# Pooling and convolution-norm stores moved to ScalarE, margin-only zeroing, and the first projection's first tile formed inside its norm

## The reference: what is computed

```python
# first block, per layer
h = layer_norm(x) * (1 + scale) + shift          # scale, shift: rows of a modulation  silu(c) @ mod_w + mod_b
u = h @ w_in                                     # 33 tiles of 128 columns: pooling, rwkv, hgrn, gate
y_pool = pooled average minus u, times pool_w, pool_scale
# second block, first layer
h = rms_norm(x) * (1 + scale) + shift ;  u = h @ w_in
y_a = silu(layer_norm(dwconv(a_val * sigmoid(a_gate))))      # "conformer" part, 512 channels
q, k = axial_rope(rms_norm(q)), axial_rope(rms_norm(k))      # 5 tiles of 128 rows, latent and context
# later modulations: silu(c_2) @ w_ada + b_ada  (3072 columns for each of two layers)
```

## Time and profile before

| | us |
|---|---|
| median of 3 runs | 5943.3 |
| the profiled execution, its own time | 5948.01 |
| span of the profile | 5946.2 |
| TensorE busy | 5146.7 (87%) |
| VectorE busy | 3381.0 (57%) |
| ScalarE busy | 1907.4 (32%) |
| GpSimd busy | 1754.7 (30%) |

### The profile page before, as it was taken

How to read it: one execution, slowest core, us unless ns; L and a number is a source line. 1 busy time by engine, 2 the same in 40 slices (tenths; PEclk the granted TensorE clock), 3 DMA queues, 4 the chain that set the end, 5 groups by cost and what they waited for, 6 DMA issues and landing times. The chain is left out here.

```text
span 5946.2 us, 127543 instructions
## 1 busy us (share of the span) xinstructions
PE 5146.7 (87%) x55385; PEld 3991.0 (67%) x55385; DVE 3381.0 (57%) x5084; ACT 1907.4 (32%) x3021; POOL 1754.7 (30%) x1377
## 2 busy tenths in 40 slices
PE   6699999899996666487999867999988899989989
PEld 1488888788885555366888634555557788776667
DVE  2236656344443766577698257888864300058877
ACT  1224444323333443133211223444430300026652
POOL 1201111445443555024100004666642511100012
PEclk8899999899998888788999988999999899989999
DMA  6324444221212010465322331000045321141035
GB/s 205 104 95 156 151 149 150 89 65 52 67 52 89 23 57 27 149 208 151 99 107 94 134 118 44 22 17 17 13 153 166 105 74 71 61 141 39 31 114 162
DMA packets 430429, 568.20 MB, mean 96 GB/s; under 512 B 66918, under 2 KB 318694, under 8 KB 417214
## 3 DMA queue, kind: packets, MB, share of 16 engines
q1 hardware_dynamic: 365128, 387.17, 20.8%
q10 hardware_dynamic: 49542, 115.68, 5.1%
q0 software_dynamic: 15216, 57.44, 2.4%
HBM read 357.07 MB, written 203.12 MB: 94 GB/s over the span
## 5 line engine op out<-in xcount | busy, mean ns | idle before, releaser
L157 PE MATMUL p_bank<-p_hT_high,p_w_high 128*128 128x512 f32 (+1 forms) x2784 | 1052.6, 378 | 21.1 <-DVE p_w_low L151 16.8
L159 PE MATMUL p_bank<-p_hT_high,p_w_low 128*128 128x512 f32 (+1 forms) x2784 | 1044.3, 375 | 0.0
L158 PE MATMUL p_bank<-p_hT_low,p_w_high 128*128 128x512 f32 (+1 forms) x2784 | 1044.1, 375 | 0.0
L157 PEld LDWEIGHTS p_bank<-p_hT_high,p_w_high 128*128 128x128 f32 x2784 | 524.9, 189 | 124.1 <-DVE p_w_low L151 17.5
L159 PEld LDWEIGHTS p_bank<-p_hT_high,p_w_low 128*128 128x128 f32 x2784 | 524.8, 189 | 95.2
L158 PEld LDWEIGHTS p_bank<-p_hT_low,p_w_high 128*128 128x128 f32 x2784 | 525.2, 189 | 93.0
L2860 POOL TENSOR_TENSOR at_acc<-at_acc,at_p 128x512 f32<-128x512 f32 x256 | 425.3, 1661 | 144.3 <-ACT at_p L2798 122.5
L2798 ACT ACTIVATE at_p<-at_sc 128x1024 f32<-128x1024 f32 (+1 forms) x296 | 284.9, 1013 | 400.8 <-PE at_sc L2689 349.0
L1530 PE MATMUL rsc_db<-rsc_W,rsc_TK 64*64 64x64 f32 x8640 | 385.5, 220 | 6.2 <-issue 5.7
L2902 DVE TENSOR_REDUCE at_mx<-at_mb 128x2 f32<-128x1024 f32 (+1 forms) x280 | 342.2, 1222 | 83.1 <-PE at_mb L2700 81.1
L157 PE MATMUL o_bank<-o_w_high,o_m_high 128*128 128x512 f32 x800 | 314.4, 393 | 63.5 <-POOL o_m_low L151 63.5
(11 more groups left out here) (420 smaller groups left out, 10676.7 us busy)
## 6 DMA issues: line engine op xcount, KB each, us to landing
rsc_X<-rwkv_chunks SPq DMA_DIRECT2D x108, 320.0 KB, 4.7
pT<-p_o ACTq DMA_DIRECT2D x132, 256.0 KB, 2.2
rwkv_chunks<-p_arr POOLq DMA_DIRECT2D x54, 512.0 KB, 5.4
o_z<-pT SPq DMA_DIRECT2D x50, 512.0 KB, 5.4
o_y<-y SPq DMA_DIRECT2D x50, 512.0 KB, 7.0
pT<-p_eo ACTq DMA_DIRECT2D x96, 256.0 KB, 2.0
p_w<-in_w_in_dram SPq DMA_DIRECT2D x33, 512.0 KB
x<-o_o ACTq DMA_DIRECT2D x32, 512.0 KB, 2.6
```

Of the source, the lines that this page charges most:

```text
L157: nc.tensor.matmul(out, lhs[0], rhs[0], start=start, stop=False)
L158: nc.tensor.matmul(out, lhs[0], rhs[1], start=False, stop=False)
L159: return nc.tensor.matmul(out, lhs[1], rhs[0], start=False, stop=stop)
```

## The change

Four edits.

1. **One tile of the first projection is formed in its norm.** With `later` given, `EARLY` is 1. The tile is `rwkv[0] + 9`, the first of `project_rwkv`'s list. Its weights are loaded right after x(0) into `hf[0]`, which is free until tile 0, and split by GpSimd ahead of its loop into `w_part[0]`, which `project_rwkv` now gets as `first_part` and uses for odd n (even n use the one pair it makes itself). ScalarE waits for that split before it writes `hf[0]` in round 0. TensorE forms the tile in quarters (6 matmuls, two k each) after `piece(t - 1)` in rounds t = 5 to 17, 13 of 20 quarters, and 7 after the loop. ScalarE copies a chunk out in rounds 9, 13, 17 and stores it one round later, from one buffer `eo`; the last two chunks follow the loop. At the end ScalarE waits until all five stores have landed. The weights of tile 1 of the projection are loaded in the norm too (round 13, into the free `mw[0]`) and split by ScalarE and VectorE at its end into the same `w_part[0]`, once the last quarter has read it. `project_rwkv` starts at n = 1.
2. **`mo` has one buffer in place of two.** `biased(q)` now waits until the store of piece q-1 has landed; before it waited for that of q-2.
3. **Pooling zeroes only the margins.** Four memsets of 128 x 32 x 8 and one of `wd` take the place of two of 128x2560 and that of `wd`.
4. **Stores on ScalarE.** Pooling's two stores are issued by ScalarE after its fourth and eighth scaling, the conformer's five at the end of each `gate`; both wait for ScalarE's own last instruction. `first.stores(sp)` is gone from SyncE's list.

```diff
-    for n in range(M):
-        if n >= 1:
-            sp.wait_ge(w_split, n)
+    for n in range(2, M):
+        if n >= 3:
+            sp.wait_ge(w_split, n - 2)
...
-        EARLY = 0 if later else 2
-        if EARLY:
+        EARLY = 1 if later else 2
+        if later:
+            COLS = [(rwkv[0] + 9, True)]
+            NEXT = rwkv[0] + 10
+            w_part = [[s.sb(f"w0_{part}", [P, KT, P], F32R) for part in ("high", "low")]]
+            w_full, w_high, w_split = s.sems("w0_full", 2), s.sem("w0_high"), s.sem("w0_split")
+            NO = 1
...
+            SHARES = 4 // EARLY
+            HALVES = [(u, h) for u in range(len(UNITS)) for h in range(SHARES)]
...
+            if later:
+                w_sb, eo = [hf[0]], [s1.sb("eo", [P, NT])]
...
+                mo = s1.sb("mo", [2, MC])
+                w_next = mw[0][:, :, 0:P]
...
+                        if later and t == len(PIECES) + 1:
+                            sp.wait_ge(mw_free, len(PIECES))
+                            sp.dma_start(w_next, wv[:, :, NEXT * P:(NEXT + 1) * P]).then_inc(w_full[1], 16)
...
+                        elif later and t == 0:
+                            act.wait_ge(w_split, 1)
...
+                        if later and t >= LAG + 4 and (t - LAG - 4) % 4 == 0:
+                            early_out((t - LAG - 4) // 4)
+                        if later and t >= LAG + 5 and (t - LAG - 5) % 4 == 0:
+                            early_store((t - LAG - 5) // 4)
...
+                    if later:
+                        early_store((N - LAG - 4) // 4)
+                        for c in range((N - LAG - 4 + 3) // 4, PER_TILE):
+                            early_out(c)
+                            if c == PER_TILE - 1:
+                                act.wait_ge(w_full[1], 16)
+                                nc.scalar.copy(w_part[0][0][:], w_next).then_inc(w_high, 1)
+                            early_store(c)
+                        act.wait_ge(e_out[0], 16 * PER_TILE)
...
-                        if q >= 2:
-                            dve.wait_ge(mo_out[q % 2], q // 2 * 16)
-                        nc.vector.tensor_tensor(mo[q % 2][:], mp[q % 2][0:2, 0:MC], mb[q % 2][:], ALU.add).then_inc(mo_full, 1)
+                        if q:
+                            dve.wait_ge(mo_out[(q - 1) % 2], (q + 1) // 2 * 16)
+                        nc.vector.tensor_tensor(mo[:], mp[q % 2][0:2, 0:MC], mb[q % 2][:], ALU.add).then_inc(mo_full, 1)
...
+                    if later:
+                        dve.wait_ge(w_high, 2)
+                        split_low(nc.vector, w_part[0][1][:], w_next, w_part[0][0][:]).then_inc(w_split, 1)
...
-        sp.wait_ge(self.zeroed, 3)
+        sp.wait_ge(self.zeroed, 5)
...
-        for b in (self.u[0], self.u[1], self.wd):
-            self.nc.vector.memset(b[:], 0.0).then_inc(self.zeroed, 1)
+        for u in self.u:
+            for pad in (slice(0, POOL_PAD), slice(POOL_PAD + self.W, WP)):
+                self.nc.vector.memset(u[:, :, pad], 0.0).then_inc(self.zeroed, 1)
+        self.nc.vector.memset(self.wd[:], 0.0).then_inc(self.zeroed, 1)
...
                 self.nc.scalar.activation(self.out(t)[:, c * NT:(c + 1) * NT], self.ps[c][:], ACT.Copy, scale=self.sc[:, t:t + 1]).then_inc(self.scaled, 1)
+            act.wait_ge(self.scaled, 4 * (t + 1))
+            act.dma_start(self.yT[t * P:(t + 1) * P, 0:SEQ], self.out(t)).then_inc(self.stored, 16)
...
-                first.stores(sp)
...
         x.then_inc(self.acted, 1)
+        act.wait_ge(self.acted, c + 1)
+        t0 = self.CHUNKS[c][0]
+        act.dma_start(self.rows[:, :, t0:t0 + n], self.y[c][:, :, 0:n]).then_inc(self.stored, 16)
```

More of the change, by code:

```diff
@@ L159, in split_product, with project_rwkv @@
     return nc.tensor.matmul(out, lhs[1], rhs[0], start=False, stop=stop)
-def project_rwkv(nc, s, hT, wv, out, chunks_lat, row0, shift, w0, w_up, a0, a_up, k_k, k_a, r_k, head_ones, seg, R, E, bonusT, saved):
+def project_rwkv(nc, s, hT, wv, out, chunks_lat, first_part, row0, shift, w0, w_up, a0, a_up, k_k, k_a, r_k, head_ones, seg, R, E, bonusT, saved):
     W = 2 * P
@@ L194, in project_rwkv @@
     w_sb = s.sb("w0", [P, KT, P])
-    w_part = [[s.sb(f"w{u}_{part}", [P, KT, P], F32R) for part in ("high", "low")] for u in range(2)]
+    w_part = [[s.sb(f"w1_{part}", [P, KT, P], F32R) for part in ("high", "low")], first_part]
     w_full, w_high, w_split = s.sem("w_full"), s.sem("w_high"), s.sem("w_split")
@@ L531, in _ @@
             dve.wait_ge(prm_ready, 1)
-            for n in range(2, LEAD):
+            for n in range(3, LEAD):
                 split(n)
@@ L656, in _ @@
                             load_x(t + NX)
-                        if EARLY and t in (4, 6):
+                        if later and t == len(PIECES) + 1:
+                            sp.wait_ge(mw_free, len(PIECES))
+                            sp.dma_start(w_next, wv[:, :, NEXT * P:(NEXT + 1) * P]).then_inc(w_full[1], 16)
+                        if not later and t in (4, 6):
                             n = EARLY + (t - 4) // 2
@@ L875, in _ @@
                             half(t - 1)
-                        if EARLY and t >= LAG + 4 and (t - LAG - 4) % 4 == 0:
+                        if not later and t >= LAG + 4 and (t - LAG - 4) % 4 == 0:
                             early_out((t - LAG - 4) // 4)
@@ L1316, in out @@
         return self.u[t][:].rearrange("p r w -> p (r w)")[:, 0:SEQ]
-    def stores(self, sp):
-        for t in range(2):
-            sp.wait_ge(self.scaled, 4 * (t + 1))
-            sp.dma_start(self.yT[t * P:(t + 1) * P, 0:SEQ], self.out(t)).then_inc(self.stored, 16)
     def finished(self, sp):
@@ L2397, in loads @@
             sp.dma_start(self.pr[:, j, :], v.rearrange("(t p) -> p t", p=P), allow_slow_non_contiguous=True).then_inc(self.par_in, 16)
-    def stores(self, sp):
-        for c, (t0, n) in enumerate(self.CHUNKS):
-            sp.wait_ge(self.acted, c + 1)
-            sp.dma_start(self.rows[:, :, t0:t0 + n], self.y[c][:, :, 0:n]).then_inc(self.stored, 16)
     def finished(self, sp):
```

55 lines of the change are left out of this document (27 added, 28 removed).

## The result

| | before | after |
|---|---|---|
| median of 4 runs, us | 5942.94 (5938.39 to 5953.5) | 5896.26 (5892.46 to 5903.38) |
| the profiled execution, its own time | 5948.01 | 5892.46 |
| span of the profile | 5946.2 | 5890.7 |

The ratio after to before is 0.992, with a 95% interval of 0.9904 to 0.9935. The medians differ by 46.7 us, the two profiled executions by 55.6. The surplus is not the change's: between the first projection's end and pooling (rwkv and hgrn scans, the same code in both) before took 1317.1 us and after 1308.8, and over all twelve profiled executions of this case that stretch went from 1301.9 to 1322.1 with no order by kernel. So what follows is measured inside the touched stages, from one event of a stage to another, and not on the span.

A forecast was written before the change was run, and what follows sets the result against it. TensorE was busy 5146.7 of 5946.2 us, so the gain lay in its idle time. First norm and projection 22.6, margins 3.5 and conformer 20.6 sum to 46.7 us: 5943.3 - 46.7, taken as 5897, range 5885 to 5914.

The forecast's parts named there:

- the tile that goes: First projection: one tile with a chunk of 256 is removed, saving 24.7 us less any later start of TensorE.
- (a): Start of the first norm: one more 512 KB load ahead of the constants, its split hidden; +0.6 us.
- (b): First norm's rounds: quarters and single mo mostly covered or absorbed, two-tile period stays 20.3 us; +2.7 us after the last piece.
- (c): End of the first norm: last split, last four quarters, copy, store, barrier; TensorE starts the projection at 248.7, 2.1 us later.
- Edit 3: Pooling's start: zeroing only margins costs 1.4 to 1.9 us against 5.14, so loads and first add come earlier; gain 3.5 us.
- Edit 4, pooling: Pooling's stores: ScalarE issues them while it has nothing to do, and SyncE does not gain; 0 us.
- Edit 4, conformer: Conformer stage: pieces issued before the stores, item 3's load earlier; 22.2 us less 1.65 for ScalarE's issues, gain 20.6 us.
- items 4 to 9 keep their distance: Conformer stage: these items' loads wait for stores that come earlier by as much, so item 3's 22.2 us carries through.
- B: First norm: single mo paces it, stores landing at 5.4 us in both halves, costing 10 us; 5907 us, chance 0.17.
- C: First norm: TensorE is never free when quarters come, so the early tile is worth 8 us; 5911 us, chance 0.09.
- D: Conformer stage gives only 10 us: pieces collide with table and item loads, or ScalarE's issues stall; 5907 us, chance 0.07.
- E: First projection: granted clock falls without the 16.84 us pause, slower than before; 5957 us at a 0.92 grant, chance 0.02.

The follow-up runs named there:

- n_one_mo: The kernel before with only mo cut to one buffer, no quarters in the norm: 5944.8 us, ratio 0.9990 to 1.0009.
- n_quarters_late: After with all 20 quarters behind the norm's loop, none between its rounds: 5914.8 us, norm 199.8 us.
- n_send_first: After with GpSimd's store of a piece's result issued ahead of its split of the same round: 5890.7 us, norm 174.6 us.
- c_undo: After with the conformer's five stores back on SyncE ahead of the four pieces' loads: 5916.3 us, conformer stage 207.5 us.
- n_norm_only: The kernel before with the early tile and the single mo buffer alone, pooling and conformer as before: 5913.2 us.
- best_two: After with GpSimd's store ahead of its split and the conformer's stores on SyncE behind the four pieces' loads: 5880.8 us.

## Why the prediction was right

The forecast of 5897 met 5896.3, and the sum of 46.7 us the 46.7 between the medians. That the two agree to a tenth of a us is luck: the interval of the ratio alone leaves 39 to 57 us, and two terms were wrong by 2 to 3 us with opposite signs. The mechanisms of the three large terms (the tile that goes, the margins, the queue of the conformer stage) are right.

- **Edit 1, the tile that goes (24.7).** Right. The projection went from 840.4 to 815.8, 24.6 us, and between 814.1 and 815.8 in all runs with it.
- **Edit 1 (a) and (b), the rounds (+0.6, +2.7).** Wrong in size. The norms of after's order take 182.8 to 184.6 us over five profiles, 184.0 in the mean; the two profiles without the early tile 182.6 and 185.3, 184.0 in the mean. Nothing is lost. The start is in fact later, by 1.4 us and not 0.6 (first transposes 14.62 us behind x(0), 13.21 before), and the step's picture of the rounds, one half covered and the other absorbed, did hold in n_one_mo. What the step did not see is that the quarters would lift TensorE's clock and shorten pieces and transposes. It took the store of the quiet half to land in some 2 us because it is issued ahead of the next piece's load. That holds where the clock is not lifted (1.7 us in n_quarters_late, for a store at 156.2 ahead of the load at 156.6). In after the shorter products let the load go first, the store lands after 5.3 to 6.0 us in both halves, and the loop through the one `mo` sets every round. The two do not add: a pair takes some 20.3 us with the lower clock alone (before), with the lower clock and the wait (n_one_mo, n_quarters_late) and with the wait alone (after), and some 18 with neither (n_send_first).
- **Edit 1 (c), the tail.** Right in its chain (last split, last quarters, copy, landing or low part of the weights, barrier), 8.1 us where it summed to 7.3. The last 24 products took 4.3 us and not 2.9 (239.68 to 244.01, behind 1.79 us of idleness; they start 0.12 us apart at first and 0.21 from 241.07 on). Copy, cast and low part took 2.6 more, to 246.62, where 2.4 was forecast, and from there TensorE starts after 1.1 us and not 1.99. TensorE starts at 247.68 with an x(0) load 2.5 us later in this profile: 1.5 us earlier behind it than before, where 2.1 later was forecast.
- **Edit 3 (3.5).** Right: 3.8 to pooling's first add, five pieces of some 0.27 as the row of `wd` had it. Pooling's second store still has the 3.8 (issued 50.9 us behind the memset before, 47.1 with the margins, in the mean). That the first add itself stood at 2382.7 and not at the 2392 of the forecast is the scans' doing.
- **Edit 4, pooling (0).** No run undid it alone. The stage, from memset to the next stage's first load, went from 153.9 us (mean of three profiles, 153.3 to 154.5) to 151.7 (nine, 149.9 to 154.1): 2.2 us, less than the 3.8 of the margins. So a gain from these stores is not seen, and a cost of one or two us can't be excluded.
- **Edit 4, conformer (20.6).** The mechanism is right: load at 5.6 us behind the store, no wait of 26 us, c_undo 18 to 20 us slower. The size is 17.7 (208.1 over four profiles, 190.4 over five); with SyncE's late stores it is 20.5 (187.6 over three). ScalarE's two stores ahead of the fourth reciprocal of the conformer cost 1.2 us as forecast (1.1): it comes 11.2 us behind the third and not 10.0. At item 3's reciprocal the two traces are 18.3 us apart. What failed is "items 4 to 9 keep their distance" and that the steps keep their length. Item 4's gather takes 6.5 us in place of 3.72, so that reciprocal 3 to reciprocal 4 is 16.9 to 17.1 with ScalarE's stores and 14.2 to 14.3 before and in the runs on SyncE (15.9 in n_norm_only); items 5 to 9 give 1.5 back. The spread of item 0 takes 5.25 us where it took 3.72, but that is nearly covered. These are products at the lower clock, which a sum of durations copied from the trace of before can't hold.
- **Rivals.** B's mechanism (the single `mo` paces the norm, its store landing late in both halves) is there in after, with a price of 0 against before, because it only hides what the higher clock would have given; taking it out is worth 8.1 us of norm in the mean. C is excluded by n_quarters_late, D by c_undo, E by the grant of 1.00 over the projection.

I had put B at +10 and expected of it a longer time; that a pacing mechanism can be true and cost nothing against before was not among the cases.

## What to carry to other kernels

When an issuing queue is late, look at what it waits for in front of the late transfer, and move the transfers that need no wait ahead of it; which engine issues mattered little here. When idle time is filled with products, the products around them can get faster too, and the next limit, here a store that waited behind a split although its data was ready, then takes that gain unless it is moved as well. Measure a 10 us edit inside its own stage: untouched stages of this kernel moved by 20 us from one execution to the next.

## What the runs showed of the hardware

- Filling gaps lifted the granted clock: 0.83 in the norm's rounds from 135 to 195 us without quarters (before, n_one_mo, n_quarters_late), 0.97 to 1.00 with them, the same 16 products of 128x384 at 6.6 to 7.3 us every second time against 5.32 each time in after.
- The same gather of 16 products after the same 3.65 us of idleness took 3.72 or 6.5 us, at a granted clock of 1.00 (best_two) or 0.57 (after). Which of the two a run takes does not go by the order of the stores alone, and the cause is open.
- A 3 KB store from GpSimd landed 5.3 to 6.0 us after its issue when a 1.5 MB load was under way at its issue (seven stores of after's norm), and 1.6 to 1.8 when none was (the five others); 256 KB stores from ScalarE in the same norm landed in 2.2 us by the median.
- Stages with the same code and the same data, the scans, took 1301.9 to 1322.1 us.
